# Differential attention's scores, one map after the other in place of alternating halves of the partitions

## The reference, cut to what matters

```
k1, k2 = kt[..., 0, :], kt[..., 1, :]
def block(qblk):                       # 128 queries of one head
    s1 = einsum('bhqd,bhkd->bhqk', qblk[..., 0, :], k1) * scale
    s2 = einsum('bhqd,bhkd->bhqk', qblk[..., 1, :], k2) * scale
    w = softmax(s1) - lam * softmax(s2)
    return einsum('bhqk,bhkd->bhqd', w, vt)
```

## Time and profile before

| | |
|---|---|
| median of 3 runs | 3139.05 us (3134.72 to 3148.21) |
| time of the profiled execution | 3138.06 us |
| its span on the core | 3136.4 us |
| TensorE matmuls busy | 2782.4 us (89%) |
| VectorE, ScalarE busy | 1788.2 us (57%), 1242.2 us (40%) |
| score matmuls at L2126 | 384, first at 312.4 us, last at 506.6 us |

### The profile page before, as it was taken

The page is one execution under the profiler, slowest core; times in us unless marked ns, Lnnn a source line. Parts: engine busy times, 40 slices in busy tenths (PEclk is TensorE's granted clock), DMA queues, the critical chain, the costliest instruction groups (busy, mean ns, idle before and its releaser), DMA issues. The chain is left out here.

```text
span 3136.4 us, 57152 instructions
## 1 busy us (share of the span) xinstructions
PE 2782.4 (89%) x22094; PEld 2184.6 (70%) x22094; DVE 1788.2 (57%) x3365; ACT 1242.2 (40%) x2263; POOL 308.6 (10%) x461
## 2 busy tenths in 40 slices
PE   7998896888977999999878999978888999968888
PEld 6787564666846877788666888765557888855557
DVE  4762777787251222222255677468865667559874
ACT  4332564676141010000065322258852332248861
POOL 0000564000021222222100000000000000000000
PEclk9999998899988999999989999979999999978989
DMA  5222763311376999999965123351035223260024
GB/s 184 88 74 74 230 167 124 106 41 49 108 278 244 377 377 382 378 381 378 342 220 174 68 101 111 107 182 28 1 121 171 78 84 111 82 213 25 14 79 143
DMA packets 226699, 509.23 MB, mean 162 GB/s; under 512 B 29376, under 2 KB 102016, under 8 KB 201824
## 3 DMA queue, kind: packets, MB, share of 16 engines
q1 hardware_dynamic: 202736, 448.67, 39.9%
q0 software_dynamic: 22640, 58.01, 6.8%
q10 hardware_dynamic: 1152, 0.27, 0.0%
HBM read 414.14 MB, written 93.66 MB: 162 GB/s over the span
## 5 line engine op out<-in xcount | busy, mean ns | idle before, releaser
L1912 PE MATMUL ps<-w_up,ex_xT 128*32 128x384 f32 x3072 | 344.2, 490 | 15.8 <-DMA w_up<-in_w_dram 14.9
L1914 PE MATMUL ps<-w_up,ex_xT 128*32 128x128 f32 x3072 | 348.5, 274 | 0.0
L1914 PEld LDWEIGHTS ps<-w_up,ex_xT 128*32 128x32 f32 x3072 | 332.1, 110 | 0.6
L1863 DVE TENSOR_TENSOR ex_hid<-ps,ex_act 32x128 f32<-32x128 f32 x96 | 28.2, 294 | 301.8 <-PE ps L1914 301.0
L910 ACT CAST next_w<-early 128x512 fp32r<-128x512 f32 x128 | 79.7, 623 | 256.6 <-PE ps L1224 219.4
L1939 PE MATMUL ps<-w_down,ex_hT 128*32 128x512 f32 (+1 forms) x1536 | 172.0, 487 | 5.4 <-DVE ex_y L1877 2.8
L1941 PE MATMUL ps<-w_down,ex_hT 128*32 128x256 f32 x768 | 172.2, 380 | 0.0
L1011 DVE TENSOR_TENSOR next_w<-early,next_w 128x512 fp32r<-128x512 f32 x128 | 88.3, 690 | 134.6 <-ACT next_w L910 133.7
L682 PE MATMUL ps<-mix_in_wh,mix_in_xh 128*128 128x512 f32 x384 | 152.6, 398 | 7.3 <-DVE mix_in_xl L462 3.8
L683 PE MATMUL ps<-mix_in_wl,mix_in_xh 128*128 128x512 f32 x384 | 151.0, 393 | 0.0
L684 PE MATMUL ps<-mix_in_wh,mix_in_xl 128*128 128x512 f32 x384 | 150.6, 392 | 0.0
(11 more groups left out here) (507 smaller groups left out, 7448.2 us busy)
## 6 DMA issues: line engine op xcount, KB each, us to landing
w_up<-in_w_dram SPq DMA_DIRECT2D x128, 1024.0 KB
w_down<-in_w_dram SPq DMA_DIRECT2D x64, 1024.0 KB
proj<-in_st SPq DMA_DIRECT2D x112, 256.0 KB, 2.0
da_w_ada<-in_w_ada_dram SPq DMA_DIRECT2D x32, 768.0 KB, 4.4
in_right<-in_w_in_dram SPq DMA_DIRECT2D x16, 1024.0 KB, 5.4
early<-in_w_in_dram SPq DMA_DIRECT2D x14, 1024.0 KB, 5.4
proj<-mix_in_out SPq DMA_DIRECT2D x48, 256.0 KB, 2.0
early<-in_w_in_dram SPq DMA_DIRECT2D x4, 2048.0 KB, 12.0
```

The lines of the kernel that those rows point to most:

```text
L1912: pe.matmul(o[group(g), :], tokens[g], wh[j][:, q, 0:HM], start=first, stop=end)
L1914: last = pe.matmul(o[BR:P, g * HQ:(g + 1) * HQ], tokens[g], wh[j][:, q, HM:], start=first and g == 0, stop=end, skip_group_check=True)
```

## The change

`score` loops over the maps on the outside. For map 0 it waits for `exped[0]` alone, and then issues that map's six matmuls (three products, for each both banks), all on partitions 0 to 63; then it waits for `exped[1]` and issues the six of map 1 on partitions 64 to 127. Each map's last matmul signals `scored[c]`, as before. The same 12 matmuls with the same operands are made; no instruction of another engine is changed.

```diff
             def score(i):
                 h, t = divmod(i, NT)
-                if i > 0:
-                    pe.wait_ge(exped[0], i)
-                    pe.wait_ge(exped[1], i)
                 if t == 0:
                     pe.wait_ge(lowered, 4 * (h + 1))
-                for n in range(2):
+                for c in range(2):
+                    half = slice(c * DQK, (c + 1) * DQK)
+                    if i > 0:
+                        pe.wait_ge(exped[c], i)
                     for i_pass, (q, kk) in enumerate(((q_hi, k_hi), (q_lo, k_hi), (q_hi, k_lo))):
-                        for c in range(2):
-                            half = slice(c * DQK, (c + 1) * DQK)
+                        for n in range(2):
                             last = pe.matmul(psS[c][:, n * CH:(n + 1) * CH], q[h % 2][half, t * P:(t + 1) * P],
                                              kk[h % 2][half, n * CH:(n + 1) * CH], start=(i_pass == 0), stop=(i_pass == 2))
-                            if n == 1 and i_pass == 2:
-                                last.then_inc(scored[c], 1)
+                    last.then_inc(scored[c], 1)
```

## The result

| | before | changed |
|---|---|---|
| median | 3140.38 us (16 runs) | 3152.73 us (16 runs) |
| profiled execution's span | 3136.4 us | 3153.5 us |
| TensorE matmuls busy | 2782.4 us | 2801.2 us |

The changed kernel takes 1.0041 times as long, 95% interval 1.0034 to 1.0049: about 12 us more. Forecast were 33 us more, with a range whose lower end, 3161, the result misses. The sign was right; the size was off by a factor of about 2.7, and by the 0.5% bound the result is "the same", to which the prediction gave 0.05.

What follows compares the result with a forecast made beforehand. TensorE's queue was taken to bound the steady stretch. Longer scores +36.2, vanished waits -2.0 and the first three scores -1.0 gave +33.2 us on 3138.06, 3171.3, or 3172 us as the median; range 3161 to 3187.

Steps and rivals of the forecast that it cites:

- TensorE is the bound, a pair costs one slot: Steady tiles: TensorE's queue sets the 5.76 us period; two matmuls, one of each half, take 0.23 us like one.
- A slot of one half alone is 0.23 us, and its weight loads are hidden: Score: 64-row matmuls of one half in succession start 0.23 us apart, as full-height ones do, with loads covered by streaming.
- Rival (a): Score: weight loads into the streaming half are exposed, 1.0 us more a score, 29 us in all, 3201 us; chance 0.05.
- The border between the maps: Within a score: map 1's first matmul starts while map 0's last streams, 0.10 us after that one's start.
- The term of +1.25 us a score: Scores 3 to 31: each takes 2.83 to 2.85 us in place of 1.60, over 29 scores +36.2 us.
- its lower bound, +1.15: Least cost of a steady score: five slots more, if map 1's first weight load is covered too.
- (d): Steady tiles: something other than TensorE is the period and covers half the cost, +17 us, 3156 us; chance 0.04.
- Waits of 2.0 us that go where the heads change: Score line in each later head: three waits of 0.67 us for exponentials vanish, -2.0 us.
- The 0.92 for da_k_lo: A head's first score: this 0.92 us wait stays, since its whole chain moves with the transposes.
- The first three scores, -1: Phase start, mostly at the lower clock: separate waits and map 1's delay about cancel; -1 us taken, between -3.7 and +1.
- VectorE's maxima at the same offset: Steady tiles: the first maximum still starts 1.70 us after the score's start; the pair ends at about 4.1 us.
- rival (b): Steady scores: with half the array's rows in use the clock falls, 70 us more, 3242 us; chance 0.03.

Runs made afterwards that it cites:

- kernel on one half: Against the kernel before: both maps' scores computed on partitions 0 to 63, wait split as in the changed kernel; 3176.61 us, 1.0120 times before.
- kernels with the doubled work: Against the kernel before, both waits ahead: each map's six matmuls made twice; twelve in a run 3250.37 us (1.0346), maps alternating 3186.24 us (1.0151).

## Why the prediction was wrong

**TensorE is the bound, a pair costs one slot: right.** Every change of a score's length came out in the period: a score of 4.92 us in place of 1.60 makes the period with `turn` 9.51 in place of 6.18.

**A slot of one half alone is 0.23 us, and its weight loads are hidden: right.** The kernel on one half shows it: its twelve matmuls, each with a weight load of its own into the half that streams, start 0.23 us apart. Exposed loads would give 0.33. Rival (a) is out.

**The border between the maps: wrong, and this is the step that failed.** The prediction said: "At the border the other half is free, so map 1's first matmul can start while map 0's last is streaming." It starts with map 0's third. I took the queue's order for the order of execution, though the pairs of the earlier trace rows already showed two halves at work at once; what the rows of before could not show, since they alternate, is how far one half may run behind the queue. The term of +1.25 us a score measured +0.58, and its lower bound, +1.15, was no bound: 29 x 1.25 = 36.2 stands against some 17 that the traces have. Of the ends the prediction worked out for this term, all assumed one map nearly complete before the other begins. No rival held the right mechanism. (d) came within 4 us of the median with its 3156, by luck: it had a smaller cost for another reason, a cover by other engines, of which the traces show nothing.

**Waits of 2.0 us that go where the heads change: right** in size. Those scores start without waiting for da_e in the changed kernel (map 1 is held for under 0.1 us: the score takes 2.23 for 2.16), and with the two waits ahead the 0.67 is back. The 0.92 for da_k_lo stayed, as forecast (0.83).

**The first three scores, -1: near in size, wrong in its parts.** To score 3 it is -0.48. The prediction had map 1's delay of five slots use up what the split wait gives. The delay is two slots and hides behind map 0's maximum, so scores 1 and 2 each start about one exponential earlier (5.55 and 5.63 us after the score before, for 6.78 and 6.61). Score 2 itself takes 1.03 longer, which leaves -1.18 at `modulate`. From there to score 3 0.70 is lost, since the clock did not rise earlier, as the prediction thought it might, but is at the lower level for longer (0.76 granted over this stretch, for 0.92 before): the first eight transposes take 1.81 us, for 1.10 before.

**VectorE's maxima at the same offset: right** (1.69 for 1.70).

With the lag in place of the border, the prediction's own sum is 29 x 0.58 - 2.0 - 1.0 = +13.8 us, against +13.9 in the phase and +12.4 in the medians. That it agrees to 0.1 is in part luck, as the -1.0 stood for other things than it was made of.

## What to carry to other kernels

Matmuls that use different halves of the partitions overlap even where they don't alternate: with six of 512 columns a map they may stand in runs of up to four at no cost that showed here (1.59 us a score). A longer run costs one slot for each matmul beyond four, the first of them 0.33 us and the others 0.23; with twelve of 256 columns a map a run of four cost 0.10 already. So price a regrouping by the run's length, not by the whole of the work that no longer alternates. And where an order is new, ask how far the engine may run away from its queue before giving a bound; a bound built on one assumption about order is no bound.

## What the hardware showed that I had not expected

- TensorE starts matmuls of different halves out of the queue's order: the seventh at 353.01, the fourth at 353.23. Within a half the order stays.
- What limits it is a count of four matmuls: by theory D four sent to one half and not finished. It came out with 512 columns (map 1 starts with the third of 6 and the ninth of 12), with 256 columns (the ninth of 12), and at the lower clock too (score 0 of the changed kernel: map 0's third at 312.50, map 1's first at 312.51). That the four include the one that streams is read from these starts; what holds them in the chip is not shown.
- Whether each half has a count of its own is not shown either. A rival fits as well, one window over both halves, in which a matmul starts no earlier than the fourth one ahead of it in the queue. In every order tried here it gives the same starts: the seventh with the third, the thirteenth with the ninth, the sixth with the second. Halves with matmuls of unequal length would tell the two apart.
- The limit was tried for halves alone, not for quarters of the partitions.
- The granted clock was at times lower where one half streamed alone. The kernels with the doubled work show it (windows: stretch, us, PE, PEld, DVE, ACT, POOL busy (x), PEclk, DMA, GB/s). With twelve in a run, first at the start of the phase, then in the steady stretch:

```profile
334.60:343.60 9.00, 9.00 (x28) 6.79 (x30) 1.56 (x3) 0.00 (x0) 6.04 (x10) 0.50 0.09 7
478.00:487.00 9.00, 9.00 (x39) 6.88 (x38) 3.97 (x8) 3.74 (x7) 0.00 (x0) 0.55 0.00 1
```

With the maps alternating, at the start of the phase:

```profile
319.00:324.00 5.00, 5.00 (x24) 4.01 (x24) 0.00 (x0) 0.00 (x0) 0.56 (x1) 0.50 0.87 269
324.50:327.50 3.00, 0.00 (x0) 0.00 (x0) 2.93 (x5) 1.78 (x3) 0.00 (x0) 1.00 0.76 328
```

Behind 5 us of pairs the 2.4 GHz level was granted, while TensorE stood still. Through 9 us in which mostly one half streamed at a time the level stayed at 1.2 GHz. In the steady stretch of the run it fell once, at about 475.9, in a score whose map 0 had streamed alone from 473.65 until 475.61. That cost the profiled execution some 4 us. So rival (b)'s mechanism, dismissed with a chance of 0.03, has something to it, though it did not touch the steady stretch of the changed kernel, nor that of the kernel on one half (1.00 in both). That the empty half is the cause is an inference from these rows; no run tests it by itself.
